# Three f32 transposes behind the sum of squares on TensorE, in a two-block transformer kernel

## The reference

```
def rms_norm(x, g):
    y = xf * lax.rsqrt(jnp.mean(xf * xf, axis=-1, keepdims=True) + RMS_EPS)
    return (y * g).astype(x.dtype)

def swiglu(h, w_in, w_out):
    g, u = split_cols(h @ w_in, (D_FF, D_FF))
    return (jax.nn.silu(g) * u) @ w_out

x = x + 0.5 * swiglu(rms_norm(x, g[0]), ffn1_w_in[layer], ffn1_w_out[layer])
```

## Time and profile before

| what | value |
|---|---|
| median of 3 runs | 2282.25 us (2277.86 to 2289.23) |
| the profiled execution | 2299.78 us, span 2297.6 us |
| TensorE busy | 2221.5 us, 97% |
| DVE busy | 1522.0 us, 66% |
| ACT busy | 1183.9 us, 52% |
| POOL busy | 123.0 us, 5% |
| mean granted TensorE clock | 0.988 |
| read from memory | 389.34 MB, 170 GB/s over the span |

### The profile page before, as it was taken

How to read it: one execution, slowest core, us unless ns; L and a number is a source line. 1 busy time by engine, 2 the same in 40 slices (tenths; PEclk the granted TensorE clock), 3 DMA queues, 4 the chain that set the end, 5 groups by cost and what they waited for, 6 DMA issues and landing times.

```text
span 2297.6 us, 45005 instructions
## 1 busy us (share of the span) xinstructions
PE 2221.5 (97%) x18322; PEld 2159.6 (94%) x18322; DVE 1522.0 (66%) x2344; ACT 1183.9 (52%) x1852; POOL 123.0 (5%) x146
## 2 busy tenths in 40 slices
PE   5999998899999999999999999999999999999998
PEld 5999987799999999888999999988999999989998
DVE  5765667676667656676766666677665666667664
ACT  5644453665456444455654554545544544546543
POOL 2001000110011001000100000100000000101001
PEclk9999998999999999999999999999999999999999
DMA  7555532356565657432755665634655655535653
GB/s 239 180 181 175 161 116 65 111 188 198 192 193 173 196 187 230 138 115 74 231 189 188 198 201 186 232 102 134 194 190 172 201 184 176 182 110 169 199 193 102
DMA packets 383755, 393.29 MB, mean 171 GB/s; under 512 B 6896, under 2 KB 381808, under 8 KB 383424
## 3 DMA queue, kind: packets, MB, share of 16 engines
q1 hardware_dynamic: 381632, 383.30, 52.3%
q0 software_dynamic: 1920, 7.11, 1.1%
HBM read 389.34 MB, written 1.05 MB: 170 GB/s over the span
## 4 chain that ended last, share of the span: by engine, by line
PE 87%; DVE 5%; ACT 4%; issue 2%; POOL 1%; DMA 1%; SPq 0%; POOLq 0%; DVEq 0%; ACTq 0%
PE acc L598 25%; PE acc L599 24%; PE acc L602 24%; DVE w_lo L1373 2%; PE acc L616 2%; PE acc L618 2%; PE acc L617 2%; ACT w_hi L981 1%; PE acc L567 1%; PE acc L569 1%; PE acc L568 1%; POOL t L1880 1%; PE wide L724 1%; DMA raw<-in_ffn_w_in 1%; PE wide L779 1%
## 5 line engine op out<-in xcount | busy, mean ns | idle before, releaser
L1373 DVE TENSOR_TENSOR w_lo<-raw,w_hi 128x1024 fp32r<-128x1024 f32 (+2 forms) x790 | 898.3, 1140 | 508.6 <-ACT w_hi L981 506.0
L981 ACT ACTIVATE w_hi<-raw 128x1024 fp32r<-128x1024 f32 (+2 forms) x790 | 776.0, 988 | 819.8 <-PE acc L602 751.7
L598 PE MATMUL acc<-hn_hi,w_hi 128*128 128x256 f32 x3328 | 801.1, 282 | 25.3 <-DMA colc<-in_cols 17.8
L599 PE MATMUL acc<-hn_lo,w_hi 128*128 128x256 f32 x3328 | 793.7, 280 | 0.0
L598 PEld LDWEIGHTS acc<-hn_hi,w_hi 128*128 128x128 f32 x3328 | 631.7, 190 | 30.7 <-DMA colc<-in_cols 17.8
L599 PEld LDWEIGHTS acc<-hn_lo,w_hi 128*128 128x128 f32 x3328 | 631.6, 190 | 1.0 <-issue 0.8
L602 PE MATMUL acc<-hn_hi,w_lo 128*128 128x256 f32 x3328 | 453.2, 279 | 0.0
L602 PEld LDWEIGHTS acc<-hn_hi,w_lo 128*128 128x128 f32 x3328 | 415.8, 189 | 0.0
L599 PE MATMUL acc<-hid_lo,w_hi 128*128 128x256 f32 x1408 | 334.5, 278 | 0.0
L598 PE MATMUL acc<-hid_hi,w_hi 128*128 128x256 f32 x1408 | 334.5, 278 | 0.0
L598 PEld LDWEIGHTS acc<-hid_hi,w_hi 128*128 128x128 f32 x1408 | 265.3, 188 | 0.0
(11 more groups left out here) (253 smaller groups left out, 2254.0 us busy)
## 6 DMA issues: line engine op xcount, KB each, us to landing
raw<-in_ffn_w_in SPq DMA_DIRECT2D x88, 1024.0 KB, 5.1
raw<-in_ffn_w_out SPq DMA_DIRECT2D x32, 1024.0 KB, 5.2
raw<-in_ffn_pre_w_gate SPq DMA_DIRECT2D x22, 1024.0 KB, 5.4
raw<-in_ffn_pre_w_up SPq DMA_DIRECT2D x22, 1024.0 KB, 5.3
raw<-in_ffn_post_w_gate SPq DMA_DIRECT2D x22, 1024.0 KB, 5.4
raw<-in_ffn_post_w_up SPq DMA_DIRECT2D x22, 1024.0 KB, 5.4
raw<-in_x_w_kv SPq DMA_DIRECT2D x16, 1024.0 KB, 5.5
raw<-in_ffn_pre_w_down SPq DMA_DIRECT2D x16, 1024.0 KB, 5.2
```

The costliest lines, as they stand in the source:

```text
L598: nc.tensor.matmul(bank, wh[:, j, :], a_hi[:, u.k0 + j, :], start=u.first and j == 0, stop=False)
L599: nc.tensor.matmul(bank, wh[:, j, :], a_lo[:, u.k0 + j, :], start=False, stop=False)
L981: nc.scalar.activation(w_hi[:, u.slot, 0:u.nk, :], raw[:, u.raw % RING, 0:u.nk, P * u.half:P * u.half + P], ACT.Copy).then_inc(w_hi_ready, 1)
L1373: nc.vector.tensor_tensor(w_lo[:, u.slot, 0:u.nk, :], raw[:, u.raw % RING, 0:u.nk, P * u.half:P * u.half + P], w_hi[:, u.slot, 0:u.nk, :]. ...
```

## The change

In `sum_squares`, when no column is made, three transposes follow the sum. Each takes the first 128 tokens of one of the blocks 0 to 2 of x and writes its transpose into bank 1 of `wide`. Nothing reads what they write: the next use of that bank starts a new accumulation there.

```
@@ -640,6 +640,9 @@
                         mm = nc.tensor.matmul(wide[:, 1, 2 * t:2 * t + 2], t1[:, 0, P * t:P * t + P], ones[:, 0:2],
                                               start=True, stop=True)
                 mm.then_inc(sums_done, 1)
+                if not column:
+                    for b in range(3):
+                        nc.tensor.transpose(wide[:, 1, P * b:P * b + P], x[:, b, 0:P], ident)
```

## The result

The change makes the kernel faster. Its median is 2277.23 us over 20 runs (2269.36 to 2287.95), beside 2296.65 us over 20 runs of the kernel before (2269.63 to 2329.14); the three runs shown ahead of the prediction were among the faster ones of these. The ratio is 0.9937, 95% interval 0.9918 to 0.9956. The spread changed as well: the standard deviation of the 20 runs went from 13.9 to 5.3 us, while the fastest runs of both kernels are the same. The prediction was 2284.8 us and no measurable change. The time fell into the range, but the direction was wrong, and so was the reason.

The account below looks back on a forecast made before the run. TensorE, busy for 97% of the span, was taken as the bound. Seven busy FFN norms at 0.36 us gave 2.5 us, four idle places nothing; 2282.25 + 2.5 = 2284.8 us, range 2277 to 2295.

Parts of the forecast that it names:

- The cost at the dense places: At seven FFN norms where TensorE works without a break, three transposes add 0.36 us each, 2.5 us together.
- The lower bound taken from the change-over: If transposes took over the sum's 0.19 us change-over, a busy FFN norm would cost 0.13 us, seven 0.9 us.
- the third rival's 0.82: Transposes at the seven busy FFN norms do not overlap neighbours: 0.82 us a place, 2288.0 us in all; chance 0.07.
- The cover at the idle places: At first FFN, cross attentions and final norm, existing waits hide the transposes, cost nothing; without cover, 1.1 us for three.
- Nothing behind the dense places gives the delay back or makes it larger: After the seven busy FFN norms, later waits move along with TensorE, so the 2.5 us stays; 3.8 us of room.
- is excluded at these places, since TensorE is busy through all of them: At the seven busy FFN norms no loss can become a gain; lower bound 0.9 us of cost.
- The step that carried over the difference and not the level: Added 2.5 us to the timed median 2282.25, not to the profiled execution's 2299.78, which lay 17.5 us higher.
- The slower one: Clock falls to half behind transposes at the seven busy FFN norms: 2296.7 us, or 2308.6 with longer falls; chance 0.07.
- The faster rival: Shorter waits at first FFN and second cross attention avoid clock falls, saving 5.1 us: 2279.7 us; chance 0.11.
- the step of 0.12 us: Spacing of neighbouring matmuls taken as ordinary, subtracted when costing four transposes at 0.43 us and the sum's change-over at 0.19.

Follow-up runs that it names:

- e12: Kernel before plus the three transposes only at the first FFN, two cross attentions and final norm, repeated on another chip: 2284.17 us, ratio 1.0009.
- e1: Kernel before plus the three transposes only at the seven FFN norms where TensorE works without a break: 2275.03 us median, ratio 0.988.
- e2: Kernel before plus the three transposes only at the first FFN, two cross attentions and final norm: 2291.15 us median, ratio 0.9931.
- e11: Kernel before plus two transposes behind all 15 sums and three behind unit 23 of FFNs 0 and 2: 2274.73 us median, ratio 0.9956.

## Why the prediction was wrong

- **The cost at the dense places** was right: 0.36 us forecast, 0.33 measured (880 to 887 ns from the sum to the second matmul behind, where it was 547 to 552), so 2.3 us for the seven places. The lower bound taken from the change-over and the third rival's 0.82 were both off.
- **The cover at the idle places** held, and the work behind them started about when it did; e12 shows no change in time from them.
- **The step that failed** is "Nothing behind the dense places gives the delay back or makes it larger". With it fell the sentence that a gain "is excluded at these places, since TensorE is busy through all of them". Both looked for waits only and took the time of a busy TensorE for fixed. What the instructions did to the pace of the stream behind them was not asked, so this term of the sum stood at nothing. A stream at 117 that is turned to 113 saves 4.45 ns a matmul, so 1584 x 4.45 = 7.0 us for each FFN and more where two follow each other. In the profile of after, three of the seven places did this: the leading pairs at 504, 1114 and 2099 us ran at 117 and the streams behind the transposes at 113. At 1614, where the two profiles differ, the pair was at 113 already; there the later profile had the better draw and the transposes had nothing to turn. So comparing the two profiles alone would have credited the wrong place; the 20 runs and e1 against e2 and e12 carry the conclusion. An estimate of the size from these figures: with 29 of 56 draws at 117, seven streams save 7 x 7.0 x 29/56 = 25 us, less 2.3 us for the transposes, about 23 us; the medians differ by 19.4. On e11's chip, where before is faster, the version with transposes in more places gained 9.9.
- **The time in the range is luck.** The forecast of 2284.8 was added to a median of three runs that lies 14.4 us below that of all 20, and the missed gain made up for it.
- **The scatter was taken for noise.** The step that carried over the difference and not the level noted that the profiled execution lay 17.5 us above the median and the runs 11.4 us apart. Two or three FFNs at 117 would make that. It was the thing to explain, and the trace of before showed it: equal windows with TensorE busy throughout held 179 matmuls in five of the dense streams and 172 in two. From the kernel before, two of these seven windows, and the second of them in the kernel after:

```profile
1297.00:1317.00 20.00, 20.00 (x179) 1.00 0.70 218
1617.00:1637.00 20.00, 20.00 (x172) 1.00 0.70 219
...
1617.00:1637.00 20.00, 20.00 (x179) 1.00 0.73 228
```

  In the earlier trace rows both kinds would have shown, had a middle one been read and not the first and the last: the window from 1800 to 1809 us holds 77 matmuls where those two hold 79 and 80. And the step of 0.12 us in the earlier trace rows, used as "ordinary", was one of 117.
- **The rivals.** The slower one did not happen: the granted clock is 1.00 around all seven places. Behind the dense FFN sums, groups of two to four transposes were followed by no half clock in any profile. By the rule of the Trainium skill ("TensorE: Matmul & The Clock Gate", "Part 4: PE-mode transpose") the full clock does not engage for transposes; that cost nothing here. The faster rival was on the right side for the wrong reason: in the kernel after, the fall of the clock at the first FFN is still 6.8 us long and that at the second cross attention still 3.4, the two that it wanted away. All stretches at half clock together went from 55.4 to 53.0 us, worth 1.2 at most.

What stays open: what the two paces are in TensorE, and why sequences that keep, turn over or set them do so. No rule by number, kind or time of the instructions fits all rows of the table: one transpose behind the sum turned two of five streams at 117 to 113, and behind the sum with a column four of four. That 113 follows the sum and three transposes was so in 21 of 21 places of this program, no more. Whether the length of a wait shifts the odds (6 of 18 against 18 of 28) is not shown, since it was not varied by itself.

## What to carry to other kernels

When an engine is busy all the time, count how many instructions of one kind fit into equal windows before taking its work as fixed: a stream can have more than one pace at the same clock. If the runs of a kernel scatter by more than their waits explain, compare two profiles of the same kernel stretch by stretch before predicting any change to it. A cheap group of other instructions at the start of a long stream can set its pace, but which group does so has to be measured in place, and one transpose more or less can set the other.

## What the runs showed of the hardware

A dense stream of fp32r matmuls of 128x256, each with its own weight load, ran at 113.3 or 117.8 ns from start to start, both at a granted clock of 1.00 (2.4 GHz), and kept one of them for up to 3168 matmuls (374 us in the kernel before, with one sum in between). The Trainium skill, "TensorE: Matmul & The Clock Gate", in the section "Wait — 56ns, not 53.3ns?", gives columns divided by the clock and some 2.5 ns more from start to start, an estimate of 109 ns for 256 columns. Neither measured pace is that, and the measurement decides. Over all profiles the draw behind a wait was close to even (29 of 56 at 117). An f32 transpose of 128x128 in such a stream takes 109 ns of TensorE's time from start to start, where its duration is 273 ns.
